# Hybrid decoder layer on one core: the second one-hot in two wide operations, the gate products eight units earlier, and the first value tiles split beside the last unit products

## The chip, the cores and the metric

The kernel runs on one core of one Trainium2 chip. The metric is device time in microseconds of one execution. Three runs of the kernel before have a median of 3331.61 us (3329.48 to 3332.1). All stages run in one launch on five engines, each with its own instruction queue: TensorE (PE), VectorE (DVE), ScalarE (ACT), GpSimd (POOL) and SyncE (SP), which here only issues transfers.

## The reference, cut to what matters

The layer has a mixer half (attention and a state-space part) and a feed-forward half with 16384 experts. The change lies in the second half:

```
def peer_ffn(h, w_q, sub_keys1, sub_keys2, u_tab, v_tab):      # S = 512 rows, D = 2048, 8 heads, 16 picks each
    s1, s2 = scores of each head against 128 keys each
    v1, i1 = top_k(s1, 16);  v2, i2 = top_k(s2, 16)
    top_s, pos = top_k(v1[..., :, None] + v2[..., None, :], 16)
    ids = i1 * 128 + i2 at pos;   g = softmax(top_s)
    u = take(u_tab, ids);  act = gelu(h . u)
    out = sum over picks of g * act * take(v_tab, ids)
```

## The kernel before, in words

The 512 rows are four blocks of 128. Block 3 is computed as the reference writes it: its picked rows of both tables are gathered by POOL and used by DVE (`dot`, `add_row`). Blocks 0 to 2 (384 rows, DT) are computed densely: a gate for every row and every one of the 128 x 128 experts is built, all activations are computed, and both are multiplied. Experts go in 128 tiles of 128.

**Early units.** Before the gates are known, PE computes activations of the first 48 tiles. A tile is two units (each half of D), so there are 96 (EARLY), numbered n = 0 to 95. For each unit SP loads 128x1024 weights (L663), ACT copies their high part (L1059, `early_high`, run three units ahead), POOL subtracts to get the low part (L776), and PE multiplies (L2122, 24 matmuls of 128x384). After every second unit ACT applies gelu (L1067) and stores the tile in DRAM (`acts_ahead`, L1069).

**Selecting.** Beside the units DVE finds the picks of each block in a fixed order: select(0), gates_of(0), select(1), one_hots(0), gates_of(1), select(2), one_hots(1), gates_of(2), select(3), gates_of(3), one_hots(2). `select` is max, index and replace operations and a few wide tensor operations (L1585, L1586, L1587).

**Gate products.** The dense gates of a token are the product of two one-hot rows, 128x128 experts, the second row scaled by the gate. `one_hots(m)` builds them 8 tokens at a time, 16 times a block, in four buffers (HOTS): one wide comparison for the first one-hot (L1611), and eight small operations for the second (L1614), each comparing and scaling for one token. PE multiplies them (L2143, two batches of 8 tokens a step), ACT copies the result out of PSUM in four quarters a step (L1078, `gates_staged`), and SP stores it in DRAM (L656, `gates_by_expert`). The table GATES_AT gives the unit after which the eight steps of a block begin on PE, each behind one unit: 34, 58, 82. COLS_AT, SC_AT and EXP_AT place the smaller steps of the selecting in the same way. All these orders are written out by hand.

**Handing over.** When all is stored, SP reads back the gates of the first four experts' tiles (L699) and their activations (L681), DVE multiplies them (L1724, "made"), ACT and DVE split the product in high and low part (L1124, L1727), and PE begins the value products (L2184; a value unit is 18 matmuls of 128x512). ACT (L1111) and DVE (L1714) split the value weights. This is group "start" followed by groups "ahead", which use the stored activations, eight value units a group; after them come groups that compute activations and values. During "start" and the first "ahead" group, DVE has two dot products of block 3 (L1645, one behind the split of each of the first two value units), whose rows POOL begins to gather (L791) when the last early activation is stored.

## Time and profile before

| what | value |
|---|---|
| median of three runs | 3331.61 us |
| profiled execution | 3327.78 us, its span 3326.0 us |
| PE busy | 3159.8 us (95%) |
| DVE busy | 2387.9 us (72%) |
| ACT busy | 1060.7 us (32%) |
| POOL busy | 1033.7 us (31%) |
| mean granted TensorE clock | 0.979 |
| early units | from 999.9 to 1513.9 us |
| value products begin | 1523.4 us |

A busy share over the whole span says little about one stage. In the 40 slices of the page each slice is 83 us; the early units fill slices 13 to 18, and there DVE is busy for nine tenths, while afterwards it has slack. "Idle before" an instruction says what its engine waited for; an engine that is not the last one to arrive may wait at no cost.

### The profile page before, as it was taken

How to read it: one execution, taken by the hardware profiler on the slowest of the kernel's cores; microseconds unless marked ns; L12 is line 12 of the kernel's file. 1: busy time of each engine (PE TensorE's matmuls, PEld its weight loads, DVE VectorE, ACT ScalarE, POOL GpSimd, SP SyncE). 2: the span in 40 equal slices, each digit the busy share in tenths (PEclk: the TensorE clock that was granted, in tenths of full speed). 3: DMA queues.
4: the chain of work that ended last, by engine and by line, in shares of the span. 5: the costliest groups of instructions: out<-in, count | busy, mean ns of one | idle time of the engine just before them, and what ended most of it. 6: DMA issues, size and time to landing. Idle time of an engine off the chain costs nothing.

```text
span 3326.0 us, 44344 instructions
## 1 busy us (share of the span) xinstructions
PE 3159.8 (95%) x16336; PEld 2672.9 (80%) x16336; DVE 2387.9 (72%) x3424; ACT 1060.7 (32%) x1619; POOL 1033.7 (31%) x734
## 2 busy tenths in 40 slices
PE   6999999999799999997999999999999999999994
PEld 3776887666449999996777799999999999999983
DVE  2342564743809999994888877888888888888857
ACT  1323455421303334332232233232333332333232
POOL 0110000000006635533222323435555555545300
PEclk9999999999899999998999999999999999999997
DMA  9776113465034455466888888889899989998753
GB/s 356 276 274 221 58 57 140 165 236 182 26 125 150 148 186 175 161 207 215 288 291 289 272 280 283 302 297 343 313 335 333 343 306 337 339 329 307 285 186 120
DMA packets 277263, 792.99 MB, mean 238 GB/s; under 512 B 118224, under 2 KB 138880, under 8 KB 230784
## 3 DMA queue, kind: packets, MB, share of 16 engines
q1 hardware_dynamic: 219648, 463.74, 41.5%
q0 software_dynamic: 50560, 317.87, 25.3%
q10 hardware_dynamic: 6912, 9.44, 0.8%
q8 instruction: 94, 1.54, 0.2%
q14 instruction: 49, 0.40, 0.0%
HBM read 747.97 MB, written 43.00 MB: 238 GB/s over the span
## 4 chain that ended last, share of the span: by engine, by line
PE 78%; DVE 14%; DMA 3%; issue 2%; ACT 1%; SPq 1%; POOL 0%; DVEq 0%; ACTq 0%; POOLq 0%
PE ps L2184 27%; PE ps L2122 26%; PE ps L1854 14%; PE ps L2097 3%; DVE arena L1614 3%; PE ps L1819 2%; PE ps L1878 1%; DVE arena L1640 1%; DVE arena L1611 1%; DVE split L1714 1%; PE ps L2143 1%; PE ps L1793 1%; PE ps L1913 1%; DMA arena<-in_w_ada 1%; DVE arena L1346 1%
## 5 line engine op out<-in xcount | busy, mean ns | idle before, releaser
L2184 PE MATMUL ps<-split,w_parts 128*128 128x512 f32 x4608 | 1074.0, 393 | 37.0 <-DVE split L1714 34.2
L2184 PEld LDWEIGHTS ps<-split,w_parts 128*128 128x128 f32 x4608 | 865.3, 189 | 235.4 <-DVE split L1714 35.5
L2122 PE MATMUL ps<-h_parts,split 128*128 128x384 f32 x5376 | 947.5, 335 | 1.1 <-DVE split L1714 1.1
L2122 PEld LDWEIGHTS ps<-h_parts,split 128*128 128x128 f32 x5376 | 933.6, 188 | 5.0 <-DVE split L1714 1.7
L1111 ACT ACTIVATE split<-below_parts 128x1024 fp32r<-128x1024 f32 x416 | 441.5, 1062 | 1210.3 <-PE ps L2184 702.8
L1714 DVE TENSOR_TENSOR split<-below_parts,split 128x1024 fp32r<-128x1024 f32 x416 | 509.2, 1224 | 276.7 <-ACT split L1111 271.7
L788 POOL COPY arena<-arena 128x1 uint32 x256 | 209.4, 818 | 710.6 <-DVE arena L1664 399.6
L1202 DVE TENSOR_TENSOR win_parts<-arena,win_parts 128x512 fp32r<-128x512 f32 (+2 forms) x208 | 129.2, 630 | 309.8 <-ACT win_parts L841 301.5
L1645 DVE CUSTOM_DVE_ANT_0 arena<-arena 128x2048 f32<-128x2048 f32 x128 | 293.1, 2290 | 14.9 <-DMA arena<-in_u_tab,arena 14.9
L1664 DVE SCALAR_TENSOR_TENSOR arena<-arena 128x2048 f32<-128x2048 f32 x128 | 300.7, 2350 | 2.9 <-DVE arena L1656 2.2
L791 POOL DMA_INDIRECT arena<-in_v_tab,arena x128 | 263.4, 2058 | 104.4 <-POOL arena L788 103.0
L776 POOL TENSOR_TENSOR split<-below_parts,split 128x1024 fp32r<-128x1024 f32 x64 | 173.8, 2718 | 339.1 <-ACT split L1059 339.1
L791 POOL DMA_INDIRECT arena<-in_u_tab,arena x128 | 233.3, 1822 | 109.1 <-POOL arena L788 102.1
L1640 DVE TENSOR_TENSOR arena<-arena,ps 128x1024 f32<-128x1024 f32 x189 | 225.9, 1216 | 23.2 <-PE ps L2184 23.0
L1854 PE MATMUL ps<-win_parts,h_high_part 128*128 128x512 f32 (+1 forms) x640 | 202.5, 382 | 0.0
L841 ACT ACTIVATE win_parts<-arena 128x512 fp32r<-128x512 f32 (+2 forms) x208 | 117.5, 576 | 222.2 <-PE ps L1854 222.2
L1614 DVE TENSOR_SCALAR arena<-iota,arena 128x128 f32<-128x128 f32 x384 | 171.9, 518 | 0.0
L742 POOL DMA_DIRECT2D arena<-in_w_slices x56 | 29.9, 534 | 433.0 <-DVE win_parts L1202 432.1
L1854 PEld LDWEIGHTS ps<-win_parts,h_high_part 128*128 128x128 f32 x640 | 118.7, 189 | 42.3 <-ACT win_parts L841 17.6
L2122 PE MATMUL ps<-h_parts,w_parts 128*128 128x384 f32 x768 | 140.3, 337 | 0.9 <-PE ps L1878 0.9
L1854 PE MATMUL ps<-h_high_part,win_parts 128*128 128x512 f32 x384 | 133.0, 411 | 5.3 <-DVE h_low_part L1190 5.3
L2122 PEld LDWEIGHTS ps<-h_parts,w_parts 128*128 128x128 f32 x768 | 133.8, 189 | 1.6 <-issue 1.0
(267 smaller groups left out, 3214.9 us busy)
## 6 DMA issues: line engine op xcount, KB each, us to landing
below_parts<-in_u_units SPq DMA_DIRECT2D x256, 512.0 KB, 4.9
below_parts<-in_v_tab SPq DMA_DIRECT2D x256, 512.0 KB, 6.9
arena<-in_w_ada SPq DMA_DIRECT2D x96, 1024.0 KB, 7.4
arena<-in_w_slices POOLq DMA_DIRECT2D x56, 512.0 KB, 4.2
gates_by_expert<-arena SPq DMA_DIRECT2D x24, 1024.0 KB, 4.8
below_parts<-gates_by_expert SPq DMA_DIRECT2D x32, 768.0 KB, 9.1
arena<-in_w_out POOLq DMA_DIRECT2D x32, 512.0 KB, 5.0
acts_ahead<-arena ACTq DMA_DIRECT2D x48, 192.0 KB, 2.3
```

What stands on the lines that cost most here:

```text
L776: nc.gpsimd.tensor_tensor(part[:, 1, :], pre_raw[:, n % PRE_RAWS, :], part[:, 0, :].bitcast(F32), ALU.subtract).then_inc(pre_split, 1)
L788: nc.gpsimd.tensor_copy(idx[:, slot:slot + 1], ids[:, DB, bass.ds(pick, 1)]).then_inc(idx_copied, 1)
L791: nc.gpsimd.indirect_dma_start(out=ring[slot], out_offset=None, in_=table[:, :], in_offset=bass.IndirectOffsetOnAxis(ap=idx[:, slot:slot + ...
L1111: nc.scalar.activation(split[:, j % 2, 0, :], raw[:, j % RAWS, :], ACT.Copy).then_inc(high_done, 1)
L1614: ins = nc.vector.tensor_scalar(hot[:, 1, t, :], iota[:, :], pick_cols[:, 1, at_t:at_t + 1], pick_cols[:, 2, at_t:at_t + 1], ALU.is_equal, ...
L1640: nc.vector.tensor_tensor(row, row, wide(g.bank_of(-half if before else half, m), UNIT), ALU.add).then_inc(v_read, 1)
L1645: nc.vector.tensor_tensor_reduce(out=ring[slot], in0=ring[slot], in1=h2_now, scale=1.0, scalar=0.0, op0=ALU.mult, op1=ALU.add, accum_out=a ...
L1664: nc.vector.scalar_tensor_tensor(acc_v, ring[slot], w4[:, q:q + 1], acc_v, ALU.mult, ALU.add).then_inc(row_used, 1)
L1714: nc.vector.tensor_tensor(split[:, j % 2, 1, :], raw[:, j % RAWS, :], split[:, j % 2, 0, :].bitcast(F32), ALU.subtract)\
L1854: return nc.tensor.matmul(ps[:, bank_at, 0:cols], lhs, rhs, start=first and q == 0, stop=last and q == 2)
L2122: ins = nc.tensor.matmul(ps[:, 6 + b, 0:DT], lhs[:, cols], h2_parts[:, rhs, k, :], start=k == 0 and n == 0, stop=k == KT - 1 and n == 2)
L2184: ins = nc.tensor.matmul(ps[:, g.bank_of(half, m) + b, :], w_parts[:, buf, lhs, i, m * P:(m + 1) * P], rhs[:, b * 512:(b + 1) * 512], star ...
```

## The change

Seven edits:

1. The second one-hot is made by two wide operations over 8 tokens (a comparison, a wait for it, a multiplication in place) in place of eight small ones.
2. The gate products begin after units 32, 54 and 74; the smaller steps of the selecting are moved with them.
3. ACT copies two of a step's four quarters before the high part and gelu of that step, and two after.
4. After unit 88 SP waits for the stored gates and reads back what group "start" needs; the rest of its loads, and the gates of the next group, follow by unit 95.
5. ACT splits the four first value tiles in steps 89, 90, 93 and 94, and the first two value units in steps 94 and 95. PE has no group "start" wait any more: it waits for the last gelu only in the third part of the first value unit.
6. SP's wait for all stored activations stands behind the loads of the first "ahead" group.
7. The staging buffer of the gates and the third buffer of the early units change places in memory.

```
-EXP_AT, COLS_AT, SC_AT = (12, 28, 53, 77), (19, 43, 67), (3, 19, 45)
-GATES_AT = (34, 58, 82)
+EXP_AT, COLS_AT, SC_AT = (12, 28, 49, 70), (19, 43, 63), (3, 19, 43)
+GATES_AT = (32, 54, 74)
+HANDED = 88
+TILES_AT = (89, 90, 93, 94)
...
                     nc.vector.tensor_tensor(hot[:, 0, :, :], over(iota[:, :], 1, OH), over(pick_cols[:, 0, first:first + OH], 2, NKEY), ALU.is_equal)
-                    for t in range(OH):
-                        at_t = first + t
-                        ins = nc.vector.tensor_scalar(hot[:, 1, t, :], iota[:, :], pick_cols[:, 1, at_t:at_t + 1], pick_cols[:, 2, at_t:at_t + 1],
-                                                      ALU.is_equal, ALU.mult)
-                    ins.then_inc(hot_ready, 1)
+                    nc.vector.tensor_tensor(hot[:, 1, :, :], over(iota[:, :], 1, OH), over(pick_cols[:, 1, first:first + OH], 2, NKEY), ALU.is_equal)\
+                        .then_inc(hot_made, 1)
+                    dve.wait_ge(hot_made, first // OH + 1)
+                    nc.vector.tensor_tensor(hot[:, 1, :, :], hot[:, 1, :, :], over(pick_cols[:, 2, first:first + OH], 2, NKEY), ALU.mult)\
+                        .then_inc(hot_ready, 1)
...
             for n in range(EARLY):
+                for m in range(DB):
+                    if 0 <= n - GATES_AT[m] < GATES_FOR:
+                        gates_staged(m, n - GATES_AT[m], (0, 1))
                 if n + PRE_SPLITS < EARLY:
                     early_high(n + PRE_SPLITS)
+                if n >= EARLY - 2:
+                    unit_high(Group("ahead", 1), n - (EARLY - 2))
                 if n % 2:
                     early_gelu(n // 2)
...
                     if 0 <= n - GATES_AT[m] < GATES_FOR:
-                        gates_staged(m, n - GATES_AT[m])
+                        gates_staged(m, n - GATES_AT[m], (2, 3))
+                if n in TILES_AT:
+                    tile_high(Group("start", 0), TILES_AT.index(n))
...
+                if n == HANDED:
+                    for i in range(2):
+                        sp.wait_ge(g_stored[i], 16 * (DT // TG // 2))
+                        sp.wait_ge(acts_stored[i], 16 * GT)
+                    gates_in(Group("start", 0))
+                    for i in range(2):
+                        read_back(Group("start", 0), i)
+                if n in (HANDED + 5, HANDED + 6):
+                    read_back(Group("start", 0), n - HANDED - 3)
+                if n == HANDED + 7:
+                    gates_in(Group("ahead", 1))
...
                         for m in range(DB):
+                            if g.second and j == 0 and m == 2:
+                                pe.wait_ge(pre_gelu, AHEAD * GT)
...
-            pe.wait_ge(pre_gelu, AHEAD * GT)
```

On DVE, at the start of one_hots(0) (`arena<-iota,arena` is a comparison of the numbers 0 to 127 with picked numbers), before:

```order
L1611 TENSOR_TENSOR arena<-iota,arena 128x1024 [waits cols_ready,sc_ps,g_ps]
L1614 TENSOR_SCALAR arena<-iota,arena 128x128 x8
L1611 TENSOR_TENSOR arena<-iota,arena 128x1024 [waits g_ps]
L1614 TENSOR_SCALAR arena<-iota,arena 128x128 x8
L1611 TENSOR_TENSOR arena<-iota,arena 128x1024 [waits g_ps]
```

and now:

```order
L1633 TENSOR_TENSOR arena<-iota,arena 128x1024 [waits cols_ready,sc_ps,g_ps]
L1634 TENSOR_TENSOR arena<-iota,arena 128x1024
L1637 TENSOR_TENSOR arena<-arena 128x1024 [waits hot_made]
L1633 TENSOR_TENSOR arena<-iota,arena 128x1024 [waits g_ps]
L1634 TENSOR_TENSOR arena<-iota,arena 128x1024
L1637 TENSOR_TENSOR arena<-arena 128x1024 [waits hot_made]
```

Nothing moved in DVE's own order of blocks; a batch of 8 tokens is three wide operations in place of one wide and eight small. (L1611 is L1633 now.)

On PE, from the last gate step (L2143, now L2166) to the first value unit (L2184, now L2209); every pair of L2122 rows (now L2145) is one early unit. Before:

```order
L2143 MATMUL ps<-arena 128x128 [waits g_staged]
L2143 MATMUL ps<-arena 128x128 x3
L2122 MATMUL ps<-h2_parts,split 128x384 [waits pre_gelu,pre_split]
L2122 MATMUL ps<-h2_parts,split 128x384 x23
L2122 MATMUL ps<-h2_parts,split 128x384 [waits pre_split]
L2122 MATMUL ps<-h2_parts,split 128x384 x23
...
L2122 MATMUL ps<-h2_parts,w_parts 128x384 [waits pre_split]
L2122 MATMUL ps<-h2_parts,w_parts 128x384 x23
L2184 MATMUL ps<-split,w_parts 128x512 [waits g_staged,pre_gelu,cols_ready,w_ready,unit_split]
L2184 MATMUL ps<-split,w_parts 128x512 x17
```

and now, where 14 units stand between in place of 6:

```order
L2166 MATMUL ps<-arena 128x128 [waits g_staged]
L2166 MATMUL ps<-arena 128x128 x3
L2145 MATMUL ps<-h2_parts,split 128x384 [waits pre_gelu,pre_split]
L2145 MATMUL ps<-h2_parts,split 128x384 x23
...
L2145 MATMUL ps<-h2_parts,w_parts 128x384 [waits pre_split]
L2145 MATMUL ps<-h2_parts,w_parts 128x384 x23
L2209 MATMUL ps<-split,w_parts 128x512 [waits cols_ready,g_staged,w_ready,unit_split]
L2209 MATMUL ps<-split,w_parts 128x512 x11
L2209 MATMUL ps<-split,w_parts 128x512 [waits pre_gelu]
L2209 MATMUL ps<-split,w_parts 128x512 x5
```

The eight units that stood ahead of the last block's gate steps stand behind them now.

## Rows read from the trace of the kernel before

**Rows 1.** Stretches of the run: length, busy us (instructions) by engine, PEclk, DMA share, GB/s

```profile
1123.00:1206.00 83.00, 80.18 (x534) 79.05 (x533) 80.66 (x147) 35.25 (x52) 36.48 (x14) 1.00 0.55 182
1270.00:1344.00 74.00, 71.12 (x482) 70.00 (x482) 74.00 (x145) 30.46 (x45) 28.01 (x11) 1.00 0.56 189
1412.00:1483.00 71.00, 65.62 (x441) 64.47 (x440) 70.53 (x145) 26.98 (x41) 25.96 (x10) 0.98 0.61 209
1514.00:1540.00 26.00, 7.22 (x19) 5.46 (x20) 9.30 (x13) 5.81 (x9) 5.92 (x9) 0.65 0.69 229
```

**Rows 2.** The chain that ended last, early stage: start us, us, what

```profile
1158.90 4.17 DVE arena L1614 x8
...
1425.52 2.99 PE ps L2143 x16
...
1488.86 24.99 PE ps L2122 x144
```

**Rows 3.** Groups by line and shape: busy us, mean ns, idle before and releasers

```profile
L1614 DVE TENSOR_SCALAR arena<-iota,arena 128x128 f32<-128x128 f32 x384 | 171.9, 518 | 0.0
L1611 DVE TENSOR_TENSOR arena<-iota,arena 128x1024 f32<-128x1024 f32 x48 | 59.9, 1248 | 2.4 <-PE ps L2143 2.2 <-DVE arena L1599 0.2
L1304 DVE TENSOR_TENSOR arena<-arena 128x512 f32<-128x512 f32 x8 | 5.4, 681 | 0.0
L2143 PE MATMUL ps<-arena 128*128 128x128 f32 x768 | 96.2, 279 | 13.9 <-ACT arena L1078 11.4 <-DVE arena L1614 2.5
```

**Rows 4.** Timeline of DVE and POOL in one_hots(0): start us, us, engine, line

```profile
1189.61 2.13 DVE L1614 TENSOR_SCALAR arena<-iota,arena 128x128 f32<-128x128 f32 x8
1191.66 1.21 DVE L1611 TENSOR_TENSOR arena<-iota,arena 128x1024 f32<-128x1024 f32 x1
1192.80 4.25 DVE L1614 TENSOR_SCALAR arena<-iota,arena 128x128 f32<-128x128 f32 x8
1194.03 2.42 POOL L776 TENSOR_TENSOR split<-below_parts,split 128x1024 fp32r<-128x1024 f32 x1 [5.56 <-ACT split L1059]
```

**Rows 5.** Timeline of DVE and POOL in select(2)

```profile
1248.58 2.29 DVE L1585 TENSOR_TENSOR arena<-iota,arena 128x2048 f32<-128x2048 f32 x1 [0.26 <-DVE arena L1579]
1249.91 3.23 POOL L776 TENSOR_TENSOR split<-below_parts,split 128x1024 fp32r<-128x1024 f32 x1 [1.73 <-ACT split L1059]
1251.03 4.26 DVE L1586 TENSOR_TENSOR arena<-arena 128x2048 f32<-128x2048 f32 x1
```

**Rows 6.** Timeline of PE in gate steps

```profile
1161.69 2.02 PE L2143 MATMUL ps<-arena 128*128 128x128 f32 x16 [0.90 <-ACT arena L1078]
1163.47 4.43 PE L2122 MATMUL ps<-h_parts,split 128*128 128x384 f32 x24
...
1171.46 4.41 PE L2122 MATMUL ps<-h_parts,split 128*128 128x384 f32 x24
```

**Rows 7.** Start of one_hots(2) on DVE, and all L1614: ns min/median/max, first and last start

```profile
1412.72 1.22 DVE L1611 TENSOR_TENSOR arena<-iota,arena 128x1024 f32<-128x1024 f32 x1 [0.18 <-DVE arena L1599]
```
```profile
L1614 DVE TENSOR_SCALAR arena<-iota,arena x384: 329/336/2529, 1124.3 to 1482.4; 128x128 f32<-128x128 f32 x192
```

**Rows 8.** Timeline of all engines from the last early unit to the second value unit

```profile
1513.87 0.49 ACT L1067 ACTIVATE arena<-ps 128x384 f32<-128x384 f32 x1 [7.83 <-PE ps L2122]
...
1517.87 1.04 POOL L791 DMA_INDIRECT arena<-in_u_tab,arena  x1 [0.91 <-POOL arena L788]
...
1536.21 2.28 DVE L1645 CUSTOM_DVE_ANT_0 arena<-arena 128x2048 f32<-128x2048 f32 x1
...
1538.42 1.22 DVE L1714 TENSOR_TENSOR split<-below_parts,split 128x1024 fp32r<-128x1024 f32 x1
...
1539.69 19.77 PE L2184 MATMUL ps<-split,w_parts 128*128 128x512 f32 x72 [9.42 <-DVE split L1714]
```

**Rows 9.** POOL's gathers of u rows, from issue to landing

```profile
DMA to landing us min/median/max: 6.6/9.5/13.2
```

**Rows 10.** The transfers issued from 1516 to 1530 us: count, us to landing

```profile
arena<-in_u_tab,arena POOLq DMA_INDIRECT x2, 8.5
```

More of the change, by code:

```diff
@@ L293, in stream @@
 def stream(engine, group):
-    group(Group("start", 0))
     group(Group("ahead", 1))
@@ L656, in store_gates, with read_back, gates_in @@
                 sp.dma_start(gates_out[:, n, :, :], stage[:, n % 2, :, :]).then_inc(g_stored[n % 2], 16)
+            def read_back(g, i):
+                if not (g.kind == "start" and i < 2):
+                    sp.wait_ge(w_ready, g.val(GT, i - 1))
+                sp.dma_start(gel[:, i % 2, :], acts_out[bass.ds(g.val(GT, i), 1), :, :].rearrange("a p n -> (a p) n"))\
+                    .then_inc(gel_full[i % 2], 16)
+            def gates_in(g):
+                buf = g.c % 2
+                sp.dma_start(gm[:, buf, :, :], gates_out[:, :, bass.ds(g.val(GT), GT), :].rearrange("p a b c -> p a (b c)"))\
+                    .then_inc(gm_full[buf], 16)
             sp.wait_ge(q_ps, PH)
@@ L694, in group @@
                         sp.dma_start(to, what[0:1, :].to_broadcast([P, D])).then_inc(tail_loaded, 16)
[L695 to L703 removed]
+                if not (g.second or g.kind == "last"):
+                    sp.wait_ge(w_made, g.val(GT, -GT))
+                    gates_in(g)
                 for j, (table, i, half) in enumerate(g.units):
@@ L715, in group @@
                     sp.dma_start(raw[:, slot, :], what.rearrange("a p n -> (a p) n")).then_inc(raw_full[slot], 16)
+                if g.second:
+                    for i in range(2):
+                        sp.wait_ge(acts_stored[i], 16 * (AHEAD * GT // 2))
             stream(sp, group)
@@ L1075, in gates_staged @@
                     act.wait_ge(g_stored[n % 2], 16 * (n // 2))
-                for q in range(TG // 4):
+                for q in quads:
                     act.wait_ge(g_ps, n * TG // 4 + HOTS * OH // 4 + q + 1)
@@ L1083, in _, with tile_high, unit_high @@
                 early_high(n)
+            def tile_high(g, i):
+                act.wait_ge(w_made, g.val(GT, i + 1))
+                nc.scalar.activation(w_parts[:, g.c % 2, 0, i, :], gel[:, i % 2, :], ACT.Copy).then_inc(w_high, 1)
+            def unit_high(g, j):
+                act.wait_ge(raw_full[j % RAWS], g.unit(0) * 4 + (16 * (j // RAWS + 1)))
+                if g.second and j < 2:
+                    act.wait_ge(pre_used, EARLY - 2 + j)
+                else:
+                    act.wait_ge(unit_used, g.unit(j - 1))
+                nc.scalar.activation(split[:, j % 2, 0, :], raw[:, j % RAWS, :], ACT.Copy).then_inc(high_done, 1)
             for n in range(EARLY):
+                for m in range(DB):
+                    if 0 <= n - GATES_AT[m] < GATES_FOR:
+                        gates_staged(m, n - GATES_AT[m], (0, 1))
                 if n + PRE_SPLITS < EARLY:
                     early_high(n + PRE_SPLITS)
+                if n >= EARLY - 2:
+                    unit_high(Group("ahead", 1), n - (EARLY - 2))
                 if n % 2:
@@ L1100, in _ @@
                     if 0 <= n - GATES_AT[m] < GATES_FOR:
-                        gates_staged(m, n - GATES_AT[m])
+                        gates_staged(m, n - GATES_AT[m], (2, 3))
+                if n in TILES_AT:
+                    tile_high(Group("start", 0), TILES_AT.index(n))
             def group(g):
-                buf = g.c % 2
                 for j in g.steps():
-                    if g.units:
-                        act.wait_ge(raw_full[j % RAWS], g.unit(0) * 4 + (16 * (j // RAWS + 1)))
-                        if not (g.second and j < 2):
-                            act.wait_ge(unit_used, g.unit(j - 1))
-                        nc.scalar.activation(split[:, j % 2, 0, :], raw[:, j % RAWS, :], ACT.Copy).then_inc(high_done, 1)
+                    if not (g.second and j < 2):
+                        unit_high(g, j)
                     if j == (3 if g.second else 0) and g.sums():
```

39 lines of the change are left out of this document (8 added, 31 removed).

## The prediction

> **What bounds the kernel now.** The page's busy shares say PE (95%), but the change touches only the early stage and its end, so I read that stage by itself: stretches first, then the chain of waits, then the timelines of DVE beside POOL. In the stretches the reader is to see that DVE is busy for 80.7 of 83, 74.0 of 74 and 70.5 of 71 us while it makes one-hots [rows 1]. The chain of waits runs through DVE there (L1614) until 1425.5, and only then through PE [rows 2]. So two engines share the bound: DVE sets when the last block's one-hots can begin (1412.7) and PE has placed its units so that it just keeps up. PE loses 13.9 us to waits in the gate products, 11.4 of it to ACT [rows 3]. The early units end at 1488.86 + 24.99 = 1513.85. From there to the second value unit on PE (1539.69) pass 25.8 us, of which only one value unit (4.2 us at full clock) is work: at most 21.6 us are to be had in this gap, plus what the granted clock costs, whose mean is 0.65 there [rows 1, 2, 8].
>
> **The one-hot batch.** A batch of 8 tokens takes DVE 1.14 us for the first comparison (1191.66 to 1192.80) and 2.05 for the eight small ones (1189.61 to 1191.66), 3.19 in all, when nothing is in its way [rows 4]. The mean of a small one is 518 ns against a median of 336 [rows 3, 7], so eight seem to cost 4.1 us and two wide ones only 2.3. But the excess is not theirs: with a POOL subtraction in between, the same eight take 4.25 [rows 4], 2.12 more, which is one POOL subtraction's length less a part. The question is whether wide operations escape that. They don't: the multiplication L1586, begun while POOL works, takes 4.26 us for 2048 elements where its neighbour L1585 of the same size takes 2.29, and POOL's subtraction that came during L1585 took 3.23 in place of 2.42 [rows 4, 5]. Each waits for the other. POOL's subtractions are one a unit before and after, so each costs DVE some 2.1 us in either form.
> That leaves the pure cost. Three wide ones are 3 x 1.13, and the wait between comparison and multiplication adds 0.24 (L1585 to L1586: 2.45 from start to start, less 2.21 for 2048 elements back to back) [rows 5]: 3.63 us. So the edit adds 0.44 us a batch, 21 us over 48. For the new multiplication I take the rate of L1304, a multiplication in place with one value for 64 elements, 681 ns for 512, which is one element a cycle of 1.13 us for 1024 [rows 3]. If L1586's 4.26 were its own speed and not a wait, the new one would take 2.1, which is the upper bound; below 1.13 no such row lies.
> The Trainium skill speaks against this edit too: "VectorE: DVE Perf Modes", section "Mode 2×_2P — use both read ports for one tensor", says that a float32 tensor_scalar runs at two elements a cycle and a float32 tensor_tensor at one. The trace agrees: 2.05 us for 1024 elements in eight pieces with their overheads, against 2.27 for the two wide ones.
>
> **The three blocks on DVE.** In a gate step (one unit and two batches) DVE needed 2 x 3.19 + 2.11 = 8.49 us, and PE 7.99 (1163.47 to 1171.46) or, with the wait for ACT, about 0.9 more in every other step [rows 4, 6]. Now DVE needs 2 x 3.63 + 2.11 = 9.37. DVE is then the bound in every gate step, and the 0.9 that ACT's new order saves PE is worth nothing: I price edit 3 at 0, hidden behind DVE (without that cover it would give the 11.4 us of [rows 3]).
> Block 0 took some 82.3 us from 1123.1 (1.14 before the first L1614 [rows 7]) to about 1205.5: 51.0 pure and 14.8 times 2.11 (POOL's count there is 14 [rows 1]). Now 58.1 pure; POOL comes with every unit, 4.2 us, until the gate steps begin, about 1142.5 (unit 36 begins at 1163.5 [rows 6]; less a step of 8.9, the 3.8 of a step's products and two units), then once in 9.37: 21 us at half speed make 3 batches, the other 13 take 13 x 4.69 = 61, and the sum is 82 again. Block 1 took 74.1 (11 of POOL). Now its gate steps begin at once, so 58.1 + 7.5 x 2.11 = 73.9. So the wide form costs 14 us more in these two and POOL's slower rhythm gives the 14 back, and one_hots(2) begins where it did, at 1412.7 [rows 7]. Selecting itself is untouched.
> But PE is there earlier. Block 1's batches run from 1270 to 1344 [rows 1] and its last product ends at about 1345; 12 units of 4.165 (24.99 / 6 [rows 2]) later, at 1395, begins unit 74, and at 1399 PE wants the first batch. It gets it at 1412.7 + 3.6 = 1416: a stall of some 16 us. From there PE goes at DVE's pace. one_hots(2) takes 73.9, to 1486.6; the last product ends 2 us later, 1488.6. Before, PE had 6 units left at that point, now it has 14: 14 x 4.165 = 58.3, so the units end at 1546.9 in place of 1513.9. **Term 1: +33.0 us.** The eight units moved behind the gates are exactly the work that had covered select(3).
>
> **Handing over.** Reading back begins after unit 88. The last gates are copied at about 1490 and the first tile is due on ACT after unit 89, at 1488.6 + 8 x 4.165 = 1522; a store and a read lie between, and even at the slowest gather's 13.2 us each [rows 9] they are in time. SP's read-backs at 93 and 94 wait for w_ready and hold up the raw loads of units 94 and 95 behind them; those are wanted three units (12.5 us) ahead of PE, a wait of a unit or so fits in. So the first value unit follows the last early unit at once. The second does not: DVE has the first dot product of block 3 queued ahead of its split, and POOL gathers its rows only when the last activation is stored. In the trace the gelu begins at the units' end, 1513.87, the gather is issued at 1517.87, 4.0 later, and the first two land after 8.5 (all gathers: 6.6 to 13.2) [rows 8 to 10]. 4.0 + 8.5 + 2.3 (L1645) + 1.2 (L1714) = 16.0 against 25.8 before. **Term 2: -9.8 us**, with 6.6 or 13.2 for the landing -11.7 or -5.1. The first value unit is covered by this, and PE stands idle some 12 us, as it did for 9.4; so I keep the loss to the clock unchanged: 0; at best it is 26 x 0.35 = 9 us by the mean of 0.65 [rows 1], of which I count 7 where PE doesn't stop at all. Edits 6 and 7 add no work and free a wait that nothing stands behind: 0.
> Sum: +33.0 - 9.8 = +23.2. The profiled execution took 3327.8 us (span 3326.0, the rest around it unchanged), so 3351 for such a one; the median of the runs lies 3.8 higher, so 3354.8, say 3354.
>
> **Rivals.**
> Wide operations are not held by POOL (B). For it: L1611, wide, has a mean of 1248 against 1.21 us free, nearly never held [rows 3, 4]. Against it: it stands behind eight small ones where POOL mostly gets its turn, and L1586 is held [rows 5]. Then PE's steps of 8.0 set the pace of blocks 0 and 1, and DVE ends each four batches ahead: block 0 at 1190 in place of 1205.5, block 1 at 1315 in place of 1344; one_hots(2) begins 69 us of selecting later (1344 to 1412.7), at 1384, PE's eight steps behind it take 60 to 1447, and with 58.3 the units end at 1506, -8; with -9.8 the sum is -18, 3314. Here the Trainium skill, "GPSIMD Engine Reference", section "Specifications", states that the SBUF interface is shared and that VectorE instructions with two SBUF inputs contend, which is against B; the trace shows it in L1586.
> The last block alone runs at PE's pace (E), since POOL is idle in PE's stall: 1412.7 + 3.6 + 7 x 8.0 + 3.8 + 58.3 = 1534.4, +20.5 - 9.8 = +11: 3342.
> The handover is seamless (D): the gather is no obstacle, and 21.6 of gap and 7 of clock come back. +33.0 - 28.6 = +4: 3336, no change that can be told. Against it stands the queue order on DVE.
> The multiplication runs at half rate (C), the upper bound above: 1.0 us more a batch on DVE, 48 in all, and all of it in the bound: 3402. For it only the length of L1586, against it L1304 [rows 3, 5].
>
> **Chances.** Forecast 0.70, E 0.08, C 0.03, D 0.08, B 0.11. Slower by over 0.2% (6.7 us, about what this measurement can tell) is forecast, E and C: 0.81; within it D: 0.08; faster B: 0.11. The range from 3335 to 3366 leaves out B, C and a little of the forecast's own upper side; the forecast's own range is 3344 to 3364 (landing of the gather, 3 us either way; 1 of POOL's turns more or less in a block; PE's clock after its stall).
>
> **What would show it.** L1634 and L1637 at a mean well above 1.21 us, and POOL's L776 still stretched; a batch at 4.7 us. one_hots(2) beginning near 1412 and PE waiting some 15 us for DVE at the first gate product of block 2; the units' end near 1547; the first value unit behind it with no gap; the second about 12 us later, waiting for DVE, which waits for the gather. It is wrong if L1637 is never held and one_hots(2) begins before 1395, or if PE's second value unit starts within 5 us of the first one's end.

## The result, and the profile of the changed kernel

| | before, same occasion | changed |
|---|---|---|
| median of 5 runs | 3330.63 us (3325.81 to 3332.1) | 3344.43 us (3337.39 to 3348.52) |
| ratio, 95% interval | 1 | 1.0047 (1.0032 to 1.0063) |
| profiled execution | 3327.78 (span 3326.0) | 3348.45 (span 3346.7) |

The change makes the kernel 13.8 us slower by the medians. The profiled executions lie 20.7 apart; one kernel's executions spread by 6 to 22 us, which matters below.

The stretches of the changed kernel that answer to [rows 1] (length, busy us and instructions of PE, PEld, DVE, ACT and POOL, PEclk, DMA share, GB/s):

```profile
1123.00:1206.00 83.00, 77.64 (x524) 76.49 (x522) 82.31 (x51) 34.34 (x52) 36.55 (x12) 1.00 0.53 185
1272.00:1345.00 73.00, 60.48 (x415) 58.95 (x416) 72.01 (x53) 26.82 (x42) 20.30 (x8) 0.98 0.48 167
1409.00:1482.00 73.00, 61.39 (x413) 60.09 (x414) 71.51 (x50) 26.77 (x42) 19.66 (x8) 0.93 0.55 189
1514.00:1540.00 26.00, 26.00 (x152) 26.00 (x151) 8.11 (x9) 9.49 (x13) 11.88 (x5) 1.00 0.43 125
1542.00:1568.00 26.00, 17.03 (x65) 13.54 (x65) 10.81 (x12) 4.50 (x7) 11.00 (x12) 0.80 0.80 299
```

DVE is still full in all three blocks, with a third of the instructions. In the last block PE has fallen from 65.6 of 71 us to 61.4 of 73. The fourth stretch, idle before, is full: those are the units that were moved behind the gates. The gap lies now from 1546 on.

The groups of 990 to 1560 us by line and shape (busy us, mean ns | idle before, and what ended it), against [rows 3]:

```profile
L1634 DVE TENSOR_TENSOR arena<-iota,arena 128x1024 f32<-128x1024 f32 x48 | 97.9, 2039 | 0.0
L1637 DVE TENSOR_TENSOR arena<-arena 128x1024 f32<-128x1024 f32 x48 | 71.3, 1485 | 1.6
L2166 PE MATMUL ps<-arena 128*128 128x128 f32 x768 | 100.0, 287 | 37.9 <-DVE arena L1637 37.2 <-ACT arena L1084 0.7
```

The second comparison has a mean of 2.04 us, the multiplication 1.49; together 169.2 us, where the 384 small ones had 171.9. PE's wait for ACT has gone from 11.4 to 0.7, and its wait for DVE has grown from 2.5 to 37.2. Three rows of the sources (ns min/median/max, first and last start) say what these means are made of:

```profile
L1633 DVE TENSOR_TENSOR arena<-iota,arena x48: 1209/1219/3427, 1123.4 to 1477.8; 128x1024 f32<-128x1024 f32 x48
L1634 DVE TENSOR_TENSOR arena<-iota,arena x48: 1211/1219/3428, 1124.6 to 1478.9; 128x1024 f32<-128x1024 f32 x48
L1637 DVE TENSOR_TENSOR arena<-arena x48: 1224/1225/3316, 1128.0 to 1480.2; 128x1024 f32<-128x1024 f32 x48
```

The median is the free length, 1.22 us; some take 3.4. The timeline of DVE and POOL in block 1 (start, us, engine, line) shows which:

```profile
1288.58 1.22 DVE L1633 TENSOR_TENSOR arena<-iota,arena 128x1024 f32<-128x1024 f32 x1
1289.28 2.75 POOL L782 TENSOR_TENSOR split<-below_parts,split 128x1024 fp32r<-128x1024 f32 x1 [5.24 <-ACT split L1065]
1289.71 3.41 DVE L1634 TENSOR_TENSOR arena<-iota,arena 128x1024 f32<-128x1024 f32 x1
1293.16 1.23 DVE L1637 TENSOR_TENSOR arena<-arena 128x1024 f32<-128x1024 f32 x1
```

L1634 is 2.19 us longer than its median when POOL's subtraction came before it: a wide operation is held as the small ones are. At the end of the block and at the handover, PE (as [rows 6, 8]):

```profile
1413.39 6.85 PE L2166 MATMUL ps<-arena 128*128 128x128 f32 x32 [12.13 <-DVE arena L1637]
1435.18 2.05 PE L2166 MATMUL ps<-arena 128*128 128x128 f32 x16 [1.04 <-DVE arena L1637]
...
1541.60 4.28 PE L2209 MATMUL ps<-split,w_parts 128*128 128x512 f32 x18
...
1554.86 19.06 PE L2209 MATMUL ps<-split,w_parts 128*128 128x512 f32 x72 [8.97 <-DVE split L1736]
```

The early units end at 1541.6 (before: 1513.87); the first value unit follows without a gap; the second comes at 1554.86 (before: 1539.69), 15.2 us late.

### The profile page after: what moved, and what is told of

Same layout as the page of the kernel before. It is cut to its first block, busy times and chain, and to the rows that moved or that the text cites. A ratio compares the mean times of both kernels' runs of the same rounds, so it can differ in the third digit from the quotient of the medians.

```text
span 3346.7 us, 44080 instructions
## 1 busy us (share of the span) xinstructions
PE 3161.3 (94%) x16336; PEld 2672.8 (80%) x16336; DVE 2387.3 (71%) x3136; ACT 1060.4 (32%) x1619; POOL 1043.0 (31%) x734
## 4 chain that ended last, share of the span: by engine, by line
PE 71%; DVE 19%; DMA 4%; issue 2%; SPq 2%; ACT 1%; POOL 0%; DVEq 0%; POOLq 0%; ACTq 0%
PE ps L2209 24%; PE ps L2145 22%; PE ps L1877 14%; PE ps L2120 3%; DVE arena L1634 3%; DVE arena L1637 2%; DVE arena L1633 2%; PE ps L1842 2%; DVE arena L1662 1%; PE ps L1901 1%; DVE split L1736 1%; DMA arena<-in_w_ada 1%; DMA below_parts<-in_v_tab 1%; SPq L661 1%; DMA arena<-in_u_tab,arena 1%
## 5 line engine op out<-in xcount | busy, mean ns | idle before, releaser
L2209 PE MATMUL ps<-split,w_parts 128*128 128x512 f32 x4608 | 1071.7, 392 | 31.3 <-DVE split L1736 28.4
L2209 PEld LDWEIGHTS ps<-split,w_parts 128*128 128x128 f32 x4608 | 862.2, 188 | 230.4 <-DVE split L1736 25.8
L2145 PE MATMUL ps<-h_parts,split 128*128 128x384 f32 x5376 | 948.9, 335 | 3.3 <-DVE split L1736 1.5
L2145 PEld LDWEIGHTS ps<-h_parts,split 128*128 128x128 f32 x5376 | 933.7, 188 | 7.9 <-DVE split L1736 2.6
L797 POOL DMA_INDIRECT arena<-in_v_tab,arena x128 | 270.5, 2113 | 104.4 <-POOL arena L794 103.1
L2145 PE MATMUL ps<-h_parts,w_parts 128*128 128x384 f32 x768 | 139.3, 335 | 0.6 <-PE ps L1901 0.6
L2166 PE MATMUL ps<-arena 128*128 128x128 f32 x768 | 100.0, 287 | 37.9 <-DVE arena L1637 37.2
L2145 PEld LDWEIGHTS ps<-h_parts,w_parts 128*128 128x128 f32 x768 | 133.2, 188 | 1.1 <-POOL split L782 0.5
```

The lines of the kernel that those rows point to most:

```text
L797: nc.gpsimd.indirect_dma_start(out=ring[slot], out_offset=None, in_=table[:, :], in_offset=bass.IndirectOffsetOnAxis(ap=idx[:, slot:slot + ...
L2145: ins = nc.tensor.matmul(ps[:, 6 + b, 0:DT], lhs[:, cols], h2_parts[:, rhs, k, :], start=k == 0 and n == 0, stop=k == KT - 1 and n == 2)
L2209: ins = nc.tensor.matmul(ps[:, g.bank_of(half, m) + b, :], w_parts[:, buf, lhs, i, m * P:(m + 1) * P], rhs[:, b * 512:(b + 1) * 512], star ...
```

## The experiments

Medians of runs; each ratio is to the kernel before on the same occasion, with its 95% interval. The medians of before were 3330.15 us beside narrow_in_after, wide_in_before, tables_in_before and late_dots_in_after, 3329.8 beside mid_tables_wide and mid_tables_narrow_late_dots, and 3327.58 beside the other four. Light_pool_after has four runs, after and the two narrow ones with tables in between have five, the others ten. Distances between kernels of different occasions are a few us uncertain: after lies 17.0 us above narrow_in_after by the medians and 20 by the ratios. "First unit" and "units' end" are the times at which the first early unit begins and the last one ends on PE in the profiled execution.

| kernel | one-hot | tables | handover | us | ratio (95%) | first unit | units' end |
|---|---|---|---|---|---|---|---|
| before | narrow | old | old | 3328 to 3331 | 1 | 999.9 | 1513.9 |
| act_order_in_before | narrow | old | old, new ACT order | 3321.03 | 0.9981 (0.9969 to 0.9994) | 1000.4 | 1507.3 |
| wide_in_before | wide | old | old | 3341.7 | 1.0033 (1.0017 to 1.0049) | 999.9 | 1529.5 |
| tables_in_before | narrow | new | old | 3345.48 | 1.0044 (1.0029 to 1.006) | 997.8 | 1526.7 |
| narrow_in_after | narrow | new | new | 3327.46 | 0.9987 (0.9972 to 1.0003) | 996.0 | 1518.9 |
| after | wide | new | new | 3344.43 | 1.0047 (1.0032 to 1.0063) | 1000.3 | 1541.6 |
| late_dots_in_after | wide | new | new, dots later | 3340.71 | 1.0034 (1.0019 to 1.0049) | 999.3 | 1540.7 |
| light_pool_after | wide | new | new | 3299.61 | 0.9908 (0.9888 to 0.9927) | 995.8 | 1493.1 |
| light_pool_before | narrow | old | old | 3326.32 | 0.9994 (0.9984 to 1.0004) | 994.7 | 1504.7 |
| mid_tables_narrow | narrow | between | new | 3313.93 | 0.9958 (0.9945 to 0.9972) | 996.7 | 1508.2 |
| mid_tables_wide | wide | between | new | 3330.17 | 1.0012 (1.0002 to 1.0021) | 994.5 | 1522.1 |
| mid_tables_narrow_late_dots | narrow | between | new, dots later | 3308.59 | 0.9937 (0.9924 to 0.9951) | 1000.0 | 1511.1 |

The early stage doesn't begin at the same time in all profiled executions. Where an edit changes nothing ahead of the first one-hot, as between after and narrow_in_after, the start still differs, here by 4.3 us (after first, then narrow_in_after):

```profile
1000.26 8.58 PE L2145 MATMUL ps<-h_parts,split 128*128 128x384 f32 x48 [1.43 <-POOL split L782]
995.95 8.56 PE L2145 MATMUL ps<-h_parts,split 128*128 128x384 f32 x48 [1.44 <-POOL split L782]
```

A later time in one trace has to be read against this start, and the length from the first unit to the units' end is what an edit of this stage changes: 514.0 us before, 541.3 in the changed kernel.

### The one-hot form: narrow_in_after, wide_in_before

Edit: the changed kernel with the eight small operations again, and the kernel before with only the two wide ones. For the first:

```diff
-  nc.vector.tensor_tensor(hot[:, 1, :, :], over(iota[:, :], 1, OH), over(pick_cols[:, 1, first:first + OH], 2, NKEY), ALU.is_equal)
-  nc.vector.tensor_tensor(hot[:, 1, :, :], hot[:, 1, :, :], over(pick_cols[:, 2, first:first + OH], 2, NKEY), ALU.mult)
+  for t in range(OH):
+      nc.vector.tensor_scalar(hot[:, 1, t, :], iota[:, :], pick_cols[:, 1, at_t:at_t + 1], pick_cols[:, 2, at_t:at_t + 1], ALU.is_equal, ALU.mult)
```

narrow_in_after, expected:

> The changed kernel with the second one-hot made by eight small operations again; all else as changed. Theory (DVE sets the stage, the wide form costs it 0.44 us a batch and is held by POOL just like the small one): 48 x 0.44 = 21 us less on DVE's path, one_hots(2) begins some 10 to 14 us earlier, the early units end near 1521 in place of 1541.6, the median near 3324, that is 20 below the changed kernel. Rival 1 (the wide form is the cheaper one, 2.3 us against the 4.1 that eight times the mean of 518 ns give): some 40 to 80 us longer than the changed kernel. Rival 2 (the loss is from the schedule alone): no difference from 3344.

wide_in_before, expected:

> The kernel before with only the wide form of the second one-hot. Theory: DVE is just at the bound there (8.49 us a gate step against PE's 8.46), so most of the 21 us shows: one_hots(2) ends near 1500 in place of 1483, the time is 15 to 20 us above before, 3346 to 3351. Rival (PE bound, DVE has slack there): within 3 us of before. Rival (wide is cheaper): faster by up to 11 us, what PE waits for ACT.

Measured: narrow_in_after 3327.46, 17 us under the changed kernel and even with before. The last block's one-hots begin at 1392.7 in place of 1409.7, and the units end at 1518.87 in place of 1541.60. wide_in_before: +11.5, a few us less than I expected; its last one-hots begin at 1421.8 in place of 1412.7, its second value unit at 1555.34 in place of 1539.69. Of the 17.0 and 22.7 us between after and narrow_in_after, 4.3 were there at the first unit. The form's own part is 12.7 us by the start of block 2 and 18.4 by the units' end. With the old tables it is 9.0 and 15.7. The three blocks of one-hots are 6.1, 6.0 and 5.7 us longer with the wide form (82.6, 71.8 and 71.7 against 76.5, 65.8 and 66.0). It alone turns the rest of the change (even) into a loss. PE of narrow_in_after:

```profile
1396.05 6.48 PE L2166 MATMUL ps<-arena 128*128 128x128 f32 x32 [11.79 <-DVE arena L1636]
...
1518.87 4.28 PE L2209 MATMUL ps<-split,w_parts 128*128 128x512 f32 x18
...
1531.91 18.18 PE L2209 MATMUL ps<-split,w_parts 128*128 128x512 f32 x72 [8.77 <-DVE split L1736]
```

The stall at the first product of block 2 is there with the narrow form too, 11.8 us: it is not the form's.

### The tables alone: tables_in_before

```diff
-EXP_AT, COLS_AT, SC_AT = (12, 28, 53, 77), (19, 43, 67), (3, 19, 45)
-GATES_AT = (34, 58, 82)
+EXP_AT, COLS_AT, SC_AT = (12, 28, 49, 70), (19, 43, 63), (3, 19, 43)
+GATES_AT = (32, 54, 74)
```

> The kernel before with only the four tables changed (gate products at 32, 54, 74 and the steps that go with them); small one-hots, old hand-over. Theory: one_hots(2) can't begin before DVE has done select(3), near 1402; PE waits some 15 us there and has 14 units left behind the gates in place of 6: the early units end 12 to 16 us later than 1513.9 and the time is that much above before, 3343 to 3347. Rival (the tables cost nothing, since the same units are done in another order): within 3 us of before.

Measured: +15.3, inside what was expected. In its chain of waits (start, us, what) DVE leads until the first batch of block 2, and PE from there:

```profile
1398.77 1.23 DVE arena L1611
1399.99 2.06 DVE arena L1614 x8
1402.10 6.32 PE ps L2143 x32
```

One_hots(2) begins 13.95 us earlier than before (1398.77 against 1412.72), of which 2.1 were there at the first unit; but PE has waited 9.60 us for its first batch, and eight more units stand behind it. From the first unit to the units' end it takes 15.0 us more than before. The tables cost about as much as the wide form does.

### The handover: late_dots_in_after

The dot products of block 3 go two units later in DVE's queue, and the gelu that follows them on ACT one unit later.

```diff
-  if g.second and j < 2:
-      dot(Group("start", 0), j)
+  if g.second and j in (2, 3):
+      dot(Group("start", 0), j - 2)
...
-  if j == (3 if g.second else 0) and g.sums():
+  if j == (4 if g.second else 0) and g.sums():
```

> The changed kernel with the two dot products of the first ahead group behind the splits of the third and fourth value unit in place of the first and second (and the gelu of their sums one step later on ACT). Theory (the second value unit waits only because its split stands behind a dot product whose rows are gathered late): the second value unit follows the first one at once, 9.0 us earlier, and PE's clock doesn't fall, which gives some 3 to 7 more: 9 to 15 us below the changed kernel, 3330 to 3335. Rival (the next transfer or a weight load is late as well, or DVE is made late further on): less than 4 us gained.

Measured: 3340.71, 3.7 us under the changed kernel by the medians (4 by the ratios, whose intervals overlap): my theory's figure missed, the rival's fits. PE:

```profile
1540.72 12.44 PE L2209 MATMUL ps<-split,w_parts 128*128 128x512 f32 x54
...
1556.78 11.17 PE L2209 MATMUL ps<-split,w_parts 128*128 128x512 f32 x36 [3.62 <-DVE split L1736]
1570.80 18.50 PE L2209 MATMUL ps<-split,w_parts 128*128 128x512 f32 x72 [2.84 <-DVE split L1736]
...
1589.76 16.88 PE L2209 MATMUL ps<-split,w_parts 128*128 128x512 f32 x72 [0.45 <-DVE split L1736]
```

Three value units run without a gap, so the dot product did hold the second one. But the fourth then waits for the same gather, 3.62 us; the 2.84 further on stand in the changed kernel too (2.83 at 1576.75). The gather landed later here, 8.4 us after its issue (1544.91 to 1553.29) for 5.6: with the dot products out of the way DVE's queue moves on at once, SP issues two value loads of 512 KB from 1543.34 (from 1555.67 in the changed kernel), and the gather runs beside them. The unit that began at 1595.63 in the changed kernel begins here at 1589.76: 5.9 us, of which 0.9 were there at the units' end. Of the 9 us of idle time about 5 were to be had.

### POOL's share: light_pool_after, light_pool_before

From the fourth early unit on, POOL subtracts 64 of 1024 columns, so that these kernels leave out most of the early units' low parts.

```diff
-  nc.gpsimd.tensor_tensor(part[:, 1, :], pre_raw[:, n % PRE_RAWS, :], part[:, 0, :].bitcast(F32), ALU.subtract)
+  cut = UNIT if n < PRE_SPLITS else 64
+  nc.gpsimd.tensor_tensor(part[:, 1, 0:cut], pre_raw[:, n % PRE_RAWS, 0:cut], part[:, 0, 0:cut].bitcast(F32), ALU.subtract)
```

> The changed kernel, but POOL's subtraction of an early unit runs over 64 columns in place of 1024 (from the fourth unit on), so the low parts of the early units are left mostly undone. Theory (DVE's wide operations and POOL's subtractions each wait for the other): L1634 and L1637 fall from means of 2.04 and 1.49 us to 1.22, a batch to 3.6 us, the last block of one-hots begins some 35 us earlier, PE's stall at its first gate product is gone and the early units end at 1497 to 1506 in place of 1541.6: 35 to 45 us less, 3300 to 3310. Rival (the wide ones are slow by themselves, or held by the matmuls or transfers): means unchanged, time unchanged.

> The kernel before with the same light subtraction on POOL (low parts of the early units mostly left undone). Theory: the mean of L1614 falls from 518 ns to about 340 and DVE has slack, but PE was nearly the bound, so only what PE waited for DVE comes back: the early units end 3 to 8 us earlier, 3323 to 3328. So the same relief is worth 35 us or more in the changed kernel and under 10 here, since the changed one hangs on DVE. Rival (POOL's pace does not matter to DVE): L1614's mean unchanged.

Measured: 3299.61 for the changed kernel with little on POOL; by the ratios (1.0047 less 0.9908) that is 46 us less, and the units end at 1493.14, 48.5 earlier and somewhat before the earliest expected; 4.5 of these were there at the first unit. The kernel before comes to 3326.32, which can't be told from its 3327.58. Groups of light_pool_after:

```profile
L1634 DVE TENSOR_TENSOR arena<-iota,arena 128x1024 f32<-128x1024 f32 x48 | 59.1, 1232 | 27.4 <-PE ps L2167 27.2 <-DVE arena L1622 0.2
L1635 DVE TENSOR_TENSOR arena<-iota,arena 128x1024 f32<-128x1024 f32 x48 | 59.2, 1233 | 0.0
L1638 DVE TENSOR_TENSOR arena<-arena 128x1024 f32<-128x1024 f32 x48 | 58.9, 1227 | 1.6
L2167 PE MATMUL ps<-arena 128*128 128x128 f32 x768 | 93.9, 277 | 0.2 <-ACT arena L1085 0.2
```

and of light_pool_before:

```profile
L1615 DVE TENSOR_SCALAR arena<-iota,arena 128x128 f32<-128x128 f32 x384 | 103.3, 348 | 0.0
L2144 PE MATMUL ps<-arena 128*128 128x128 f32 x768 | 95.2, 277 | 11.5 <-ACT arena L1079 11.5
```

With little of POOL's subtraction left every form has nearly its free length (1.23 for 2.04, 1.23 for 1.49, 348 ns for 518, where the median was 336), so the excess of the means is POOL's. DVE then waits for PE (27.4 us), and PE's 37.2 us of waiting for DVE are gone. The kernel before gains little, since its PE mostly kept its pace already and its 11.5 us behind ACT stayed: its second value unit begins at 1530.40, 9.3 earlier, of which 5.2 were there at the first unit and 4.1 are left; the medians show 1.3. Where the rest went is not known. With DVE unhindered the change would be a gain of 27 us (3299.61 against 3326.32).

### ACT's order alone: act_order_in_before

The first two copies of each gate step move ahead of the early unit's rounding on ACT, the last two stay behind it, all else as before.

```diff
+  if 0 <= n - GATES_AT[m] < GATES_FOR:
+      gates_staged(m, n - GATES_AT[m], (0, 1))
   if n + PRE_SPLITS < EARLY:
       early_high(n + PRE_SPLITS)
...
-  gates_staged(m, n - GATES_AT[m])
+  gates_staged(m, n - GATES_AT[m], (2, 3))
```

> The kernel before with only ACT's order of the changed one: two of the four copies of a gate step ahead of the high part and the gelu. Theory: PE's 11.4 us of waits for ACT go, but DVE needs 8.49 us a gate step, so PE waits for DVE in their place as soon as its lead of four batches is used up: 0 to 6 us below before, 3324 to 3330. Rival (ACT is the bound there): the whole 11 us come back, 3319.

Measured: −6.5 us. The group of the gate products:

```profile
L2146 PE MATMUL ps<-arena 128*128 128x128 f32 x768 | 95.2, 278 | 8.3 <-DVE arena L1617 8.3
```

The 11.4 us of waiting for ACT [rows 3] are gone, 5.8 of them came back as waiting for DVE (2.5 to 8.3). The first value unit begins at 1516.78, 6.6 us earlier than before (1523.36), 7.1 counted from the first unit. I had priced this edit at nothing beside the wide form, which no run isolates; with the narrow form it is worth 6.5.

### Tables in between: mid_tables_narrow, mid_tables_wide, mid_tables_narrow_late_dots

If PE's early arrival and DVE's pace are what the new places cost, then places between the old and the new should keep the gain of the handover without the stall. All new edits but the wide form, and:

```diff
-EXP_AT, COLS_AT, SC_AT = (12, 28, 49, 70), (19, 43, 63), (3, 19, 43)
-GATES_AT, HANDED, TILES_AT = (32, 54, 74), 88, (89, 90, 93, 94)
+EXP_AT, COLS_AT, SC_AT = (12, 28, 53, 75), (19, 43, 67), (3, 19, 45)
+GATES_AT, HANDED, TILES_AT = (34, 58, 80), 94, (93, 94, 95, 95)
```

The third and fourth read-back and the next gates are issued behind unit 95's load.

> The changed kernel with small one-hots and gate products at units 34, 58 and 80 (the smaller steps at their old places but for EXP_AT, 75; HANDED 94, first tiles split at 93, 94, 95 and 95, the last two tiles read back and the next gates fetched after unit 95's load). Theory: PE waits less for one_hots(2), and only 8 units are left behind the gates: the early units end near 1506 in place of 1518.9 with the early tables, the hand-over stays seamless: 3314, some 13 below narrow_in_after and 16 below before. Rival (the reads no longer land in time and the first value unit waits): the gain is lost, 3325 or more.

> The changed kernel with gate products at 34, 58 and 80 as in mid_tables_narrow, but with the wide one-hots. Theory: DVE sets the stage in this schedule too, so the wide form costs what it cost with the early tables (17 us): 3331, some 17 above mid_tables_narrow, and the two parts add up. Rival (the wide form only hurts together with the early tables): within 5 us of mid_tables_narrow's 3314.

> mid_tables_narrow with the two dot products behind the splits of the third and fourth value unit. There PE waits 4.9 us for the first value unit's split and 2.0 for the second's, and the dots stand behind the first split only, so at most the 2.0 can come back: 0 to 4 us below mid_tables_narrow, 3310 to 3314. Rival (as in late_dots_in_after the wait only moves to a later unit): no difference.

Measured: 3313.93, where 3314 was expected, with the units' end at 1508.2 (1506 expected); against before on its occasion that is 13.7 less, where 16 were expected. With the wide form 3330.17, 16 more (18 by the ratios) where 17 were expected. And 3308.59 with the later dot products, the fastest version that computes everything, 21 us under before on its occasion. That is 5 us less than mid_tables_narrow by the medians and 7 by the ratios, where at most 4 were expected, but the intervals overlap, and the traces show 2.4 (the sixth value unit, counted from the first early one: 1542.57 − 999.99 against 1541.66 − 996.72). More than these 2 is not shown. PE of mid_tables_narrow, then of mid_tables_narrow_late_dots:

```profile
1513.08 6.85 PE L2210 MATMUL ps<-split,w_parts 128*128 128x512 f32 x18 [4.86 <-DVE split L1737]
...
1521.92 16.90 PE L2210 MATMUL ps<-split,w_parts 128*128 128x512 f32 x72 [1.99 <-DVE split L1737]
```
```profile
1516.00 23.73 PE L2210 MATMUL ps<-split,w_parts 128*128 128x512 f32 x90 [4.86 <-DVE split L1737]
```

The handover is not seamless here: the first value unit waits 4.86 us. But the second begins at 1521.92, 17.8 us earlier than in the kernel before (1539.69), 14.6 counted from the first unit, and with the later dots 90 matmuls, five units, run in one piece.

## Why the prediction was right, and where its sizes were off

I forecast 3354, with 3335 to 3366 for the range; the median is 3344. The sign held, and so did both mechanisms, each with its run, except that the prediction did not say what had made the old gap 25.8 us long. The sum was 9.4 too high by the medians (+23.2 against +13.8) and 2.5 by the profiled execution. At the second value unit the two terms' errors, 5.3 and 2.7, add up to 8.0. That the profiled execution came within 2.5 is luck: it lost 5.4 us later on, which nothing in the prediction had.

**The batch.** Three wide operations at their free length, one of them held 2.1 to 2.2 us where a POOL subtraction comes: as forecast. light_pool_after rules out rival C by the length of the multiplication (1227 ns) and rival B by what vanishes with POOL. But the batch was mis-sized. The forecast had 3.63 us in it, with 0.24 for the wait between comparison and multiplication, taken from L1585 and L1586 [rows 5]. The timeline of an unhindered batch:

```profile
1294.30 1.22 DVE L1633 TENSOR_TENSOR arena<-iota,arena 128x1024 f32<-128x1024 f32 x1
1295.43 1.22 DVE L1634 TENSOR_TENSOR arena<-iota,arena 128x1024 f32<-128x1024 f32 x1
1296.69 1.23 DVE L1637 TENSOR_TENSOR arena<-arena 128x1024 f32<-128x1024 f32 x1
1297.83 1.22 DVE L1633 TENSOR_TENSOR arena<-iota,arena 128x1024 f32<-128x1024 f32 x1
```

From L1633 to the next L1633 it is 3.53 us: 1.13, 1.26 and 1.14. The wait costs 0.12, not 0.24. The edit adds 0.34 a batch and 16 us in all, where I had 0.44 and 21, and the traces show 15.7 to 18.4 from the first unit to the units' end; a gate step's two batches take 9.25 (1288.58 to 1297.83) for 9.37.

**The start of the last block.** "One_hots(2) begins where it did, at 1412.7": it began at 1409.7. The reason given was that the wide form costs 14 us in two blocks and the new rhythm gives 14 back. Tables_in_before shows the second alone: blocks 0 and 1 take 76.0 and 67.7 us for 82.4 and 74.3, together 13.0 less. Narrow_in_after beside after shows the first: 12.1 more in the same two. So the cancelling is real, and each term is within 2 us of what I had. The 3.0 us come from the selecting between the blocks (gates_of(2), select(3), gates_of(3)), which I had called untouched: 65.6 us from the last one-hot before it (1344.08) to the block, where it took 68.8 before (1343.90 to 1412.72). POOL catches one wide operation less there, which is 2.0 of the 3.0. Before, then now:

```profile
1402.20 4.26 DVE L1586 TENSOR_TENSOR arena<-arena 128x2048 f32<-128x2048 f32 x1
1403.02 2.29 DVE L1608 TENSOR_TENSOR arena<-arena 128x2048 f32<-128x2048 f32 x1
```

This is the same operation, also the one that [rows 5] show in select(2) with 4.26: its length there was a wait, as I took it to be.

**Term 1, +33.0: right in mechanism, 5.3 too large.** The units ended at 1541.6, +27.7. Of the difference 3.0 is the start of the block. The other 2.3 is its length, 71.7 us (1409.71 to 1480.2 and the last multiplication) for 73.9, and 1.6 of that is the batch's 3.53 for 3.63, 16 times. The stall of "some 16" was 12.1, for the earlier start and because PE came 2 us later. What held is that a us of DVE here is a us of the units' end: counted from the first unit, after and narrow_in_after differ by 12.7 us at the block's start, by the block's own 5.7 more at the units' end (18.4), and by 18.6 at the second value unit.

**Term 2, −9.8: right in mechanism, 2.7 too small.** The second value unit waits for a split that stands behind a dot product and its gather. From the units' end to it pass 13.3 us, not 16.0. The timeline of the handover:

```profile
1545.79 1.04 POOL L797 DMA_INDIRECT arena<-in_u_tab,arena  x1 [0.91 <-POOL arena L794]
...
1551.37 2.29 DVE L1667 CUSTOM_DVE_ANT_0 arena<-arena 128x2048 f32<-128x2048 f32 x1 [12.64 <-DMA arena<-in_u_tab,arena]
...
1553.58 1.22 DVE L1736 TENSOR_TENSOR split<-below_parts,split 128x1024 fp32r<-128x1024 f32 x1
```

Issue 4.2 us after the units' end (forecast 4.0), landing 5.6 later (forecast 8.5; even the lower bound, 6.6, was too high), then 2.3 and 1.2 as forecast. The landing is the size that was off. The traces point at what else is in flight. It is 5.4 to 5.6 us in the three kernels in which SP issues nothing between the units' end and the landing (after, narrow_in_after, light_pool_after), 6.2 in mid_tables_narrow beside two read-backs of 192 KB, 8.4 in late_dots_in_after beside two loads of 512 KB, and 8.5 before beside the fetch of 768 KB of gates, issued 0.1 us after the gather. No run changes this alone.

The prediction gave 16.0 for the new gap and took 25.8 from the trace for the old, without saying what had made it. It was not the gather, which had landed by 1526.4. The operation ahead of the dot product in DVE's queue, the first product of the next group, began only at 1535.73:

```profile
1517.97 0.56 SPq L699 DMA_DIRECT2D below_parts<-gates_by_expert  x1
1535.73 0.56 DVE L1724 TENSOR_TENSOR below_parts<-below_parts 128x384 f32<-128x384 f32 x1 [12.43 <-DMA below_parts<-acts_ahead]
```

It needs the group's gates and the tile's activations. The gates among the transfers issued from 1516 to 1530 us (count, KB, us to landing):

```profile
below_parts<-gates_by_expert SPq DMA_DIRECT2D x1, 768.0 KB, 17.2
```

They were fetched behind SP's wait for the stored activations and landed at 1535.2; the activations' read-back behind them, issued at 1520.03, landed after 15.7. In the changed kernel the fetch is issued at 1525.88, 15.7 us ahead of the units' end, and lands after 8.2. So the 12.5 us of this term come from the early fetch (the end of edit 4), and only with it does the gather become what PE waits for. Edit 6 moves a wait behind which these fetches stood, so "free a wait that nothing stands behind" was not shown for it; no run separates edit 6 from edit 4.

**Clock.** Priced at 0. The mean granted clock of the 26 us with the gap is 0.80, against 0.65 before; in the stall at the gate products it now costs something too: after 12.13 us of waiting the granted clock of 1413 to 1420 is 0.53, near the lower of the two levels (1.2 of 2.4 GHz), and the first 32 gate products take 6.85 us, where the 32 begun at 1424.26 take 3.91. PE goes at DVE's pace there, so that most of this is covered. No run isolates it.

**Edit 3, priced at 0**, holds in the change as the prediction meant it: DVE was the bound (37.2 us of PE's waiting). That the wide form is the cover was not tried; act_order_in_before shows that the edit is worth 6.5 us in the kernel before, without it. The prediction's 11.4 for that case was too much, as the wait for DVE was close behind.

**What stays open.** The sums at the second value unit (+15.2) and at the next ones (1595.63 against 1581.26, and 1612.86 against 1598.52: +14.4) fit the medians' +13.8. The profiled execution then loses 5.4 more by 1943.32 (before: 1923.57), where the groups behind the early stage end. ACT waited longer for raw value weights, as the waits of the whole execution say (who <- whom: us, times, longest), of after:

```profile
ACT split L1102 <- DMA below_parts<-in_v_tab: 87.7, 23, 5.4
```

and of before:

```profile
ACT split L1111 <- DMA below_parts<-in_v_tab: 38.4, 9, 5.1
```

This varies from kernel to kernel and goes with neither edit, and the stretch from the sixth value unit to the end of these groups goes with it. It takes 359.9 to 362.8 us in the seven traces with 6 to 57 us of such waits (before: 361.3), and 364.6 to 370.7 in the five with 86 to 102 us (after: 366.6; narrow_in_after, the longest of both: 370.7 and 101.7). What sets it isn't known. With the 4 to 5 us at the first early unit it is a second reason why one profiled execution can't be compared with another to better than some us.

**Do the parts add?** Nearly. Form: +11.5 with the old tables, +17.0 with the new, +16.2 with those in between by the medians; the intervals don't separate them, and from the first unit to the units' end the traces show 15.7, 18.4 and 16.1. Tables: +15.3 alone (15.0 in the traces). The rest of the change: 3327.46 against 3345.48, −18.0. In the traces ACT's order brings the units' end 6.0 us forward there (7.1 in its own run), and the handover shortens the gap up to the second value unit by 12.6 (25.6 us in tables_in_before, 13.0 in narrow_in_after). The sum +15.3 − 18.0 + 17.0 = +14.3 is no evidence that they add, as it is a chain of differences that ends at the changed kernel by construction; that the form costs about the same under three tables is.

## What to carry to other kernels

Where two engines hold each other up, a mean length in the list of groups is not the operation's price: compare it with the median, and look in the timeline at what the other engine did during the long ones. Eight small operations that "cost" 4.1 us were 2.05 us and a wait, which the two wide ones inherited whole. Work moved off the end of one engine's queue to the other side of a wait must be priced as cover that is lost there: the eight units moved behind the gates cost what they had hidden. Before a gap is priced, ask which wait makes it now: the new one here hung on a gather, the old one on a fetch that nobody had named. When traces are compared, subtract what differed before the edit began to act. And parts of one change are worth a run each: here the form and the tables were losses, ACT's order and the handover gains, and these two alone, with tables set to suit them, made the kernel 14 us faster (21 with the dot products moved as well).

## What the runs showed of the hardware

DVE and POOL each finish the instruction that they are in and hold the other's next one, in every form tried: a subtraction of 128x1024 on POOL adds 2.1 to 2.2 us to a comparison, a small compare-and-multiply or a multiplication on DVE, and at most 14 ns in the mean are left with 64 columns. Its price is unlike in two kernels, as I had expected before these runs (35 or more against under 10): 93 lighter subtractions are worth 46 us in the changed kernel and no measurable time in the kernel before. By the Trainium skill ("SBUF — State Buffer", section "SBUF: two separate sides") the two share a pair of ports as an exclusive lock that the one which starts first has for its whole instruction; the trace agrees, with 3.41 us for L1634 begun 0.43 us after the subtraction and 1.22 for the same line without it.

A gather of 128 rows landed 5.6 us after its issue with no transfer of SP issued beside it, where the gathers of this kernel have a median of 9.8 and a highest of 13.6:

```profile
DMA to landing us min/median/max: 5.6/9.8/13.6
```

A comparison of 1024 elements starts 1.13 us after its like, though each is shown with 1.22. The multiplication, which waits for the comparison just before it on the same engine, starts 1.26 us after it. For 2048 elements the same kind of wait cost 0.24 [rows 5], so its price didn't carry over from the one pair to the other; whether the size is the reason was not tried.
